# Two-layer attention, FFN and recurrence program on one core: one block of instructions for neighbouring stages, and activations turned into tiles during the last column chunk

## The chip, the cores and the metric

The program runs on one core of a Trainium2 chip. The metric is the device time of one execution in microseconds. Before the change it is 3304.31 us, the median of three runs (3301.08 to 3310.72).

## What is computed

A residual stream of 256 tokens by 2048 columns passes through six sub-layers. Two are the mixers of the older half (several kinds of attention, each with a memory projection), then come a grouped attention, a gated FFN, a recurrent mixer and a second gated FFN. Nearly all of the arithmetic is dense products with weights that are read once:

```
for each sub-layer:
    h = rms_norm(x, gain) @ w_in          # 2048 x (6680, 6224, 3072, 2*5632, 4096)
    y = mixer(h)                          # attention, recurrence, or silu(gate) * up
    x = x + y @ w_out                     # 2048 (5632 for the FFN) x 2048
```

The products are wanted at nearly float32 accuracy. So each activation a and each weight w is split into a high part (rounded) and a low part (the rest), and three products are added: a_hi w_hi + a_hi w_lo + a_lo w_hi.

## The kernel before

**Tiling.** `T` = 256 tokens are `MT` = 2 row blocks of 128. The 2048 inner columns are `KT` = 16 tiles of 128. A weight matrix is worked in column chunks of 512 (`CHUNK`). A granule is 1 MB of weights: four inner tiles by 512 columns (in the down projection one inner tile by 2048 columns). Four granules make a chunk. SyncE loads granules into four buffers (`load`, L333), ScalarE writes the high half (`split_hi`, L373) and VectorE the low half (`split_lo`, L385), each in two halves of 128x1024, into four slots (`HL` = 4). So the two engines are at most four halves ahead of TensorE. TensorE takes 24 matmuls of 512 columns a granule (L568 in `gemm`, L1689 in `ffn_up`, L1774 in `ffn_down`).

**Stages.** `build` (L148) runs one stage after another, each in an `nc.Block()` of its own, that is, with a wait of all engines for each other at its end: a key/value projection for the memory, then `gemm` with `evac="proj"` (in), a mixer, `gemm` with `evac="resid"` (out) three times; then `ffn_up` and `ffn_down`; then `gemm` with `evac="xy"`, `rnn_mixer`, `gemm` with `evac="resid"`; then `ffn_up`, `ffn_down` and `store_x`. At the end of each stage SyncE already loads the first four granules of the next (`prefetch`, L348).

**The head of a stage.** A stage that begins with a norm has `prep=Norm(...)` (L745, a `Turn`, L680). `Turn.tensor` (L693) runs ahead of the first chunk: 32 transposes of 128x128 (L698) of the residual into all eight PSUM banks, two tiles a bank. In the first chunk ScalarE (L721) and VectorE (L735) write for each granule first the high and low halves of four activation tiles, and then the two halves of the weights. The squares for the norm (L768) follow in granules 2 and 3 of the first chunk, and the row scale is applied when the chunk is read out of PSUM.

**The end of a stage.** A chunk's sums are read out (`evacuate`, L460) two granules into the next chunk; for the last chunk of a stage, after the last matmul. In the output projections VectorE does it as an addition to the residual (L478).

**The FFN.** `ffn_up` has eleven rounds f of a gate part (PSUM banks 0, 1) and an up part (banks 2, 3). ScalarE applies Silu, VectorE multiplies (`product`, L1621), TensorE turns the product with eight transposes (`turn`, L1657, L1664, banks 4, 5) after the third granule of the next round, and ScalarE copies them out (`copy_hidden`, L1589). The last round's product, transposes and copy stand at the end of the stage. `ffn_down` has eleven rounds j of four granules; it keeps all eight banks as sums of both row blocks by 2048 columns, splits the hidden tiles into high and low parts (L1743, L1752), and adds all 2048 columns of both row blocks to the residual at the very end (L1758). `store_x` (L669) then writes 2 MB with one DMA (L674).

Of the kernel before, what the change touches and what calls it, by code (L numbers as in the profile page):

```python
# [128 lines left out]


# [17 lines left out]
def build(nc, i, out, upto=99):  # L148
    ctx = ExitStack()
    with ctx:  # L150
# [121 lines left out]
        e.gran = 0  # L272
        e.queue = plan(e)
# [3 lines left out]
        gemm(e, evac="kv", prep=Norm(e, e.PR[:, :, 0:D], GC_MEM, loaded=e.s_mem))  # L277

        gemm(e, evac="proj", prep=Norm(e, e.X[:], GC_NORM, loaded=e.s_x), post=even_heads(e))
        gemm(e, evac="resid", prep=even_mixer(e))  # L280
        if upto > 1:
            gemm(e, evac="proj", prep=Norm(e, e.X[:], GC_NORM + KT), post=odd_heads(e))
            gemm(e, evac="resid", prep=odd_mixer(e))

        if upto > 2:
            gemm(e, evac="proj", prep=Norm(e, e.X[:], GC_MIX), post=gqa_heads(e))
            gemm(e, evac="resid", prep=gqa_mixer(e))
        if upto > 3:
            ffn_up(e, Norm(e, e.X[:], GC_FFN))
            ffn_down(e)  # L290
        if upto > 4:
            gemm(e, evac="xy", prep=Norm(e, e.X[:], GC_MIX + KT))
            rnn_mixer(e)
            gemm(e, evac="resid")
        if upto > 5:
            ffn_up(e, Norm(e, e.X[:], GC_FFN + KT))
            ffn_down(e)
        store_x(e)


# [47 lines left out]
def prefetch(e, sp):  # L348
# [4 lines left out]
    for q in range(4):  # L353
        if "down" in gm:
            load(e, sp, g0 + q, e.RAW[q][:], gm["down"][:, q, :], q)
        elif "rnn" in gm:
# [4 lines left out]
        else:  # L361
            one = gm.get("gate", gm)
            w = min(CHUNK, one["cols"])
            src = one["view"](0, q, w)
# [6 lines left out]


def split_hi(e, act, g, slot, rounds, n=GRAN):  # L373


    arrived(e, act, slot, rounds)
    for b in range(2):
        free = e.s_used.at(g * 2 + b - HL + 1)
        if not isinstance(g, int) or free > 0:
            act.wait_ge(e.s_used.sem, free)  # L380
        e.nc.scalar.activation(e.WH[(2 * slot + b) % HL][:, 0:n // 2], e.RAW[slot][:, b * n // 2:(b + 1) * n // 2],  # L381
                               ACT.Copy).then_inc(e.s_hi.sem, 1)


def split_lo(e, dve, g, slot, n=GRAN):  # L385

    for b in range(2):
        s = (2 * slot + b) % HL
        dve.wait_ge(e.s_hi.sem, e.s_hi.at(g * 2 + b + 1))
        e.nc.vector.tensor_tensor(e.WL[s][:, 0:n // 2], e.RAW[slot][:, b * n // 2:(b + 1) * n // 2],  # L390
                                  e.WH[s][:, 0:n // 2].bitcast(F32), ALU.subtract).then_inc(e.s_lo.sem, 1)
# [15 lines left out]
def chunk_loop(eng, n, body):  # L407


    for c in range(min(2, n)):  # L410
        body(c, c)
    pairs = (n - 2) // 2
    if pairs > 0:
        with eng.Fori(1, pairs + 1) as j:
            for h in range(2):
                body(j * 2 + h, h)
    if n > 2 and n % 2:
        body(n - 1, (n - 1) % 2)


def gemm(e, evac, prep=None, post=None):


    nc = e.nc
    gm = e.queue.pop(0)
    full, tail = gm["cols"] // CHUNK, gm["cols"] % CHUNK
    chunks = full + (1 if tail else 0)

    loop = post is None and evac != "kv"
    g0 = e.gran  # L430
    ktiles = 4

    with nc.Block() as block:
        @block.sync
        def _(sp):
            def body(c, par, w=CHUNK):
# [3 lines left out]
            if full:  # L440

                if full > 1:
                    body(1, 1)
                pairs = (full - 2) // 2
                if evac == "kv":
                    for c in range(2, full):
                        body(c, c % 2)
# [1572 lines left out]
```

## Time and profile before

| | |
|---|---|
| median of three runs | 3304.31 us |
| span of the profiled execution | 3299.8 us |
| TensorE busy | 3103.4 us, 94% |
| VectorE busy | 1727.6 us, 52% |
| ScalarE busy | 1519.2 us, 46% |
| DMA engines, share of their time in the main queue | 50.7% |
| granted TensorE clock, mean | 0.970 |

The profile lists engines as PE (TensorE's matmuls), PEld (its weight loads), DVE (VectorE), ACT (ScalarE), POOL (GpSimd) and SP (SyncE); a q behind the name is the engine's sequencer. L568 is line 568 of the kernel. Matmuls are pipelined, so a matmul's shown duration overlaps with the next one's: what one costs is the distance between two starts. A transpose is also a matmul for TensorE.

### The profile page before, as it was taken

The numbers are of one execution on the slowest core, as the hardware profiler recorded it, in microseconds if no ns is written. First come the engines' busy times: TensorE is split into PE (matmuls) and PEld (weight loads), VectorE is DVE, ScalarE is ACT, GpSimd is POOL, SyncE is SP. The second block draws the span as 40 slices with busy tenths as digits, with TensorE's granted clock in tenths as the row PEclk, the third lists the DMA queues.
The fourth block names the chain that finished last, engine by engine and source line by source line (L and its number), as shares of the span: only waits on it lengthen the run. The fifth ranks groups of instructions, "written<-read, shape, count | busy, mean of one in ns | idle before, by whom it ended". The sixth has DMA issues, their size and how long they took to land. (4 is left out here: it accounts for less than half of the span.)

```text
span 3299.8 us, 39116 instructions
## 1 busy us (share of the span) xinstructions
PE 3103.4 (94%) x14382; PEld 2574.4 (78%) x14382; DVE 1727.6 (52%) x2313; ACT 1519.2 (46%) x2117; POOL 273.1 (8%) x330
## 2 busy tenths in 40 slices
PE   6999988999979998999999999999739999999998
PEld 5888866888878887888888788788538888887887
DVE  4565537465456566544444455544585544444554
ACT  4545435354444545444444344443654444444443
POOL 0042200036000080000000000000110000000000
PEclk9999988999979999999999999999869999999999
DMA  7555431565514552555555555565225655565553
GB/s 254 179 191 191 153 131 39 167 203 192 170 54 141 179 191 66 178 191 190 191 190 179 178 191 192 168 198 181 77 71 172 197 187 187 187 197 166 192 195 134
DMA packets 253943, 551.62 MB, mean 167 GB/s; under 512 B 13232, under 2 KB 30480, under 8 KB 241808
## 3 DMA queue, kind: packets, MB, share of 16 engines
q1 hardware_dynamic: 252592, 548.84, 50.7%
q0 software_dynamic: 384, 1.05, 0.2%
q8 instruction: 61, 1.00, 0.1%
q10 hardware_dynamic: 864, 0.39, 0.0%
q14 instruction: 42, 0.34, 0.0%
HBM read 548.14 MB, written 2.10 MB: 167 GB/s over the span
## 5 line engine op out<-in xcount | busy, mean ns | idle before, releaser
L390 DVE TENSOR_TENSOR weights_lo<-weights,weights_hi 128x1024 fp32r<-128x1024 f32 (+1 forms) x1016 | 1232.8, 1222 | 1116.7 <-ACT weights_hi L381 1115.6
L381 ACT ACTIVATE weights_hi<-weights 128x1024 fp32r<-128x1024 f32 (+1 forms) x1016 | 1055.1, 1049 | 1246.1 <-PE psum L568 617.9
L568 PE MATMUL psum<-weights_hi,act_hi 128*128 128x512 f32 (+2 forms) x1952 | 757.3, 388 | 52.7 <-DVE weights_lo L390 52.7
L568 PE MATMUL psum<-weights_hi,act_lo 128*128 128x512 f32 (+2 forms) x1952 | 756.5, 388 | 0.0
L568 PE MATMUL psum<-weights_lo,act_hi 128*128 128x512 f32 (+2 forms) x1952 | 756.5, 388 | 0.0
L1689 PE MATMUL psum<-weights_hi,act_hi 128*128 128x512 f32 x1408 | 550.0, 391 | 1.8 <-DVE weights_lo L390 1.8
L1689 PE MATMUL psum<-weights_hi,act_lo 128*128 128x512 f32 x1408 | 548.3, 389 | 0.0
L1689 PE MATMUL psum<-weights_lo,act_hi 128*128 128x512 f32 x1408 | 547.7, 389 | 0.0
L568 PEld LDWEIGHTS psum<-weights_hi,act_hi 128*128 128x128 f32 x1952 | 371.9, 191 | 127.7 <-DVE weights_lo L390 49.9
L568 PEld LDWEIGHTS psum<-weights_lo,act_hi 128*128 128x128 f32 x1952 | 372.0, 191 | 73.4
L568 PEld LDWEIGHTS psum<-weights_hi,act_lo 128*128 128x128 f32 x1952 | 372.0, 191 | 73.4
L1689 PEld LDWEIGHTS psum<-weights_hi,act_hi 128*128 128x128 f32 x1408 | 264.3, 188 | 56.4 <-issue 2.2
L1689 PEld LDWEIGHTS psum<-weights_hi,act_lo 128*128 128x128 f32 x1408 | 264.3, 188 | 55.2
L1689 PEld LDWEIGHTS psum<-weights_lo,act_hi 128*128 128x128 f32 x1408 | 264.4, 188 | 54.3
L1774 PE MATMUL psum<-weights_hi,ffn_hidden_hi 128*128 128x512 f32 x704 | 275.8, 392 | 8.7 <-DVE weights_lo L390 8.7
L1774 PE MATMUL psum<-weights_lo,ffn_hidden_hi 128*128 128x512 f32 x704 | 275.2, 391 | 0.0
L1774 PE MATMUL psum<-weights_hi,ffn_hidden_lo 128*128 128x512 f32 x704 | 275.1, 391 | 0.0
L1774 PEld LDWEIGHTS psum<-weights_hi,ffn_hidden_hi 128*128 128x128 f32 x704 | 133.0, 189 | 36.9 <-DVE weights_lo L390 9.2
L1774 PEld LDWEIGHTS psum<-weights_hi,ffn_hidden_lo 128*128 128x128 f32 x704 | 133.0, 189 | 27.8
L1774 PEld LDWEIGHTS psum<-weights_lo,ffn_hidden_hi 128*128 128x128 f32 x704 | 133.1, 189 | 27.6
L927 POOL TENSOR_TENSOR rotation_temps<-proj,shape_consts 128x128 f32<-128x128 f32 (+3 forms) x100 | 80.2, 822 | 632.9 <-DVE proj L909 598.9
L1909 POOL TENSOR_TENSOR rnn_input<-rnn_input,rnn_conv 128x512 f32<-128x512 f32 x16 | 22.9, 1441 | 1148.0 <-ACT rnn_input L1878 1148.0
(222 smaller groups left out, 1965.1 us busy)
## 6 DMA issues: line engine op xcount, KB each, us to landing
weights<-in_ffn_w_gate SPq DMA_DIRECT2D x88, 1024.0 KB, 5.2
weights<-in_ffn_w_up SPq DMA_DIRECT2D x88, 1024.0 KB, 5.1
weights<-in_ffn_w_down SPq DMA_DIRECT2D x88, 1024.0 KB, 4.8
weights<-in_even_w_in SPq DMA_DIRECT2D x52, 1024.0 KB, 5.0
weights<-in_odd_w_in SPq DMA_DIRECT2D x48, 1024.0 KB, 5.1
weights<-in_w_out SPq DMA_DIRECT2D x32, 1024.0 KB, 5.1
weights<-in_rnn_w_in SPq DMA_DIRECT2D x32, 1024.0 KB, 5.3
weights<-in_attn_w_qkv SPq DMA_DIRECT2D x24, 1024.0 KB, 5.2
```

The source lines that it names most:

```text
L381: e.nc.scalar.activation(e.WH[(2 * slot + b) % HL][:, 0:n // 2], e.RAW[slot][:, b * n // 2:(b + 1) * n // 2], ACT.Copy).then_inc(e.s_hi.se ...
L390: e.nc.vector.tensor_tensor(e.WL[s][:, 0:n // 2], e.RAW[slot][:, b * n // 2:(b + 1) * n // 2], e.WH[s][:, 0:n // 2].bitcast(F32), ALU.subt ...
L568: last = nc.tensor.matmul(e.PS[:, 2 * par + m, 0:w], a, x, start=(kk == 0 and n == 0), stop=(kk == 4 * ktiles - 1 and n == 2))
L927: mult = lambda out, a, b: e.nc.gpsimd.tensor_tensor(out, a, b, ALU.mult)
L1689: last = nc.tensor.matmul(e.PS[:, 2 * part + m, :], a, x, start=(kk == 0 and j == 0), stop=(kk == KT - 1 and j == 2))
L1774: last = nc.tensor.matmul(e.PS[:, 4 * m + 2 * h + b, :], a, x, start=(first and k == 0), stop=(final and k == 2))
L1909: nc.gpsimd.tensor_tensor(mine(e.RIX, g), mine(e.RIX, g), of(e.XC, n), ALU.mult).then_inc(e.s_input.sem, 1)
```

## The change

What is done at the joints between stages is rearranged; the products are the same.

- Stages that have no mixer between them share one `nc.Block()` (class `Flow`): kv and even in; even out and odd in; odd out and qkv; attention out, FFN up, FFN down and recurrent in; recurrent out, FFN up, FFN down and the store. Signals are read through marks (`Mark`) taken when a stage is made, so that a stage's waits stay valid while the next one is being written.
- `gemm` becomes the class `Gemm`. Its chunk loops are written out. The last chunk's read-out moves to the next stage, after its second granule (`carry_scalar`, `carry_vector`).
- The 32 transposes of the next norm go in four portions of eight (`CHUNK_LEAD`): after granules 0, 1 and 2 of the last chunk of the stage before, and after granule 1 of the new stage's first chunk. They use banks 4 to 7 twice. The high and low halves of the activations follow on ScalarE and VectorE: two groups in the last chunk, two in the new stage's first. Each portion waits for the addition of its residual columns, and for its bank's former contents to be split.
- The last round's product, transposes and copy of the FFN's up stage move into the down stage's first granule (`carry_tensor` and the others), which uses other PSUM banks first.
- The down stage's last two granules are loaded as two inner tiles by 1024 columns each. So the left 1024 columns are finished 24 matmuls before the end, and are added then (`add(dve, 0)`); the right ones are added in the next stage (`add(dve, 1)`). The next norm's transposes go in four portions: after the first and the second half of the right columns' matmuls, and after granules 0 and 1 of the next stage (`HALF_LEAD`).
- The store is four DMAs of 512 columns, each after the addition of its columns.

The core of the diff:

```diff
+        flow = Flow(e)
+        flow.add(Gemm, evac="resid", prep=turned)
+        flow.add(FfnUp, prep=Norm(e, e.X[:], GC_FFN, lead=CHUNK_LEAD))
+        flow.add(FfnDown)
+        flow.add(Gemm, evac="xy", prep=Norm(e, e.X[:], GC_MIX + KT, lead=HALF_LEAD))
+        flow.emit()
+        rnn_mixer(e)
...
+    def vector(self, dve):
+        mine = self.kind == "resid"
+        prep, post = self.prep, self.post
+        for c, w in enumerate(self.widths):
+            for q in range(4):
+                if c == 0 and prep is not None:
+                    prep.before_lo(dve, q)
+                self.split_lo(dve, c * 4 + q, q, 4 * w)
+                if q == 1 and c > 0 and mine:
+                    self.evacuate(dve, c - 1)
+                if q == 1 and c == 0 and self.prev is not None:
+                    self.prev.carry_vector(dve)
+                if c == 0 and prep is not None:
+                    prep.after_lo(dve, q)
+                if post is not None:
+                    post.vector(dve, c - 1, q)
+                if c == self.last and self.next is not None:
+                    self.next.prep.early_lo(dve, q)
...
+CHUNK_LEAD = Lead((4, 5, 6, 7, 4, 5, 6, 7), {0: 0, 1: 1, 2: 2}, {2: 0, 3: 1}, {1: 3}, {0: 2, 3: 3})
+HALF_LEAD = Lead((6, 7, 6, 7, 4, 5, 6, 7), {}, {}, {0: 2, 1: 3}, {0: 0, 1: 1, 2: 2, 3: 3})
...
+    def turn(self, pe, q):
+
+        e = self.e
+        for k in range(4 * q, 4 * q + 4):
             self.ready(pe, k)
+            b = k // 2
+            before = [x for x in range(b) if self.banks[x] == self.banks[b]]
+            if k % 2 == 0 and before:
+                pe.wait_ge(self.alo.sem, self.alo.at(before[-1] + 1))
...
     def ready(self, pe, k):
...
+        if k % 4 == 0:
+            pe.wait_ge(*self.final[k // 4])
...
+    BANK = ((0, 2), (6, 4))
...
+                    for m in range(MT):
+                        if first and h == 0 and m == 0:
+                            pe.wait_ge(up.gate.sem, up.gate.at(up.n))
+                        if first and h == 1 and m == 0:
+                            up.carry_tensor(pe)
+                        if first and h == 1 and m == 1:
+                            pe.wait_ge(up.hcopied.sem, up.hcopied.at(up.n))
+                        last = self.products(None, h, m, hh, hl, q, (2 * q + h) % HL, 0, first)
...
+        for h in range(2):
+            for k in range(2):
+                pe.wait_ge(self.lo.sem, self.lo.at(final * 8 + (2 + h) * 2 + k + 1))
                 for m in range(MT):
...
+                    last = self.products(None, h, m, hh, hl, 2 + k, (2 * (2 + h) + k) % HL, 0, final=(k == 1))
+                last.then_inc(self.used.sem, 1)
+                if h == 1 and self.next.prep is not None:
+                    self.next.prep.turn(pe, k)
...
+        for q in range(4):
+            cols = slice(q * CHUNK, (q + 1) * CHUNK)
+            sp.wait_ge(*self.final[q])
+            sp.dma_start(dst[:, :, cols], e.X[:, :, cols]).then_inc(self.out.sem, 16)
+        sp.wait_ge(self.out.sem, self.out.at(4))
```

The four dictionaries of a `Lead` are: granule of the old stage's last chunk to portion transposed, the same for the activation halves, and both for the new stage's first chunk.

## Rows read from the trace of the kernel before

**Rows 1.** Page, busy us of each engine, share of the span, instructions.
```profile
PE 3103.4 (94%) x14382; PEld 2574.4 (78%) x14382; DVE 1727.6 (52%) x2313; ACT 1519.2 (46%) x2117; POOL 273.1 (8%) x330
```

**Rows 2.** TensorE's waits: who for whom, us in total, times, longest us.
```profile
PE psum L568 <- DVE weights_lo L390: 52.7, 5, 49.5
PE psum L636 <- DMA cmp_w<-in_nsa_cmp_w: 22.0, 1, 22.0
...
PE psum L1774 <- DVE weights_lo L390: 8.7, 2, 4.4
...
PE psum L698 <- PEq L433: 7.9, 5, 1.6
...
PE psum L698 <- PEq L1723: 4.8, 1, 4.8
...
PE psum L1664 <- DVE ffn_hidden L1629: 3.0, 2, 1.5
```

**Rows 3.** Timeline, TensorE at the joint before the second FFN: start, duration, instruction, [idle].
```profile
2544.45 0.39 PE L568 MATMUL psum<-weights_hi,act_lo 128*128 128x512 f32 x1
2544.67 0.39 PE L568 MATMUL psum<-weights_hi,act_hi 128*128 128x512 f32 x1
...
2545.13 0.39 PE L568 MATMUL psum<-weights_hi,act_lo 128*128 128x512 f32 x1
2547.09 3.69 PE L698 MATMUL psum<-shape_consts,resid 128*128 128x128 f32 x32 [1.58 <-PEq L433]
2551.68 0.47 PE L1689 MATMUL psum<-weights_hi,act_hi 128*128 128x512 f32 x1 [0.90 <-DVE weights_lo L390]
```

**Rows 4.** Timeline, VectorE and ScalarE at the same joint.
```profile
2545.55 1.22 DVE L478 TENSOR_TENSOR resid<-resid,psum 128x1024 f32<-128x1024 f32 x1 [8.56 <-PE psum L568]
2548.64 1.66 DVE L735 SCALAR_TENSOR_TENSOR act_lo<-psum,gain_cols,act_hi 128x256 fp32r<-128x256 f32 x4 [1.87 <-ACT act_hi L721]
2550.31 2.36 DVE L390 TENSOR_TENSOR weights_lo<-weights,weights_hi 128x1024 fp32r<-128x1024 f32 x2
...
2547.77 1.57 ACT L721 ACTIVATE act_hi<-psum,gain_cols 128x256 fp32r<-128x256 f32 x4 [12.04 <-PE psum L698]
2549.21 2.02 ACT L381 ACTIVATE weights_hi<-weights 128x1024 fp32r<-128x1024 f32 x2
...
2558.41 1.89 ACT L768 ACTIVATE squares<-resid 128x2048 bf16<-128x2048 f32 x1
2560.22 0.18 ACT L768 ACTIVATION_READ_ACCUMULATOR squares<-resid 128x1 f32 x1
```

**Rows 5.** Timeline, TensorE where the FFN's loop turns a hidden chunk.
```profile
1446.91 1.04 PE L1664 MATMUL psum<-shape_consts,ffn_hidden 128*128 128x128 f32 x8
1447.71 0.47 PE L1689 MATMUL psum<-weights_hi,act_hi 128*128 128x512 f32 x1
1448.02 0.39 PE L1689 MATMUL psum<-weights_lo,act_hi 128*128 128x512 f32 x1
```

**Rows 6.** Timeline, TensorE from the first FFN's up to its down stage.
```profile
1874.83 0.39 PE L1689 MATMUL psum<-weights_hi,act_lo 128*128 128x512 f32 x1
1876.72 1.09 PE L1664 MATMUL psum<-shape_consts,ffn_hidden 128*128 128x128 f32 x8 [1.50 <-DVE ffn_hidden L1629]
1882.17 0.80 PE L1774 MATMUL psum<-weights_hi,ffn_hidden_hi 128*128 128x512 f32 x1 [4.36 <-DVE weights_lo L390]
...
1886.54 0.40 PE L1774 MATMUL psum<-weights_lo,ffn_hidden_hi 128*128 128x512 f32 x1
```

**Rows 7.** The same in the second FFN.
```profile
3046.91 0.80 PE L1774 MATMUL psum<-weights_hi,ffn_hidden_hi 128*128 128x512 f32 x1 [4.36 <-DVE weights_lo L390]
...
3050.46 0.40 PE L1774 MATMUL psum<-weights_hi,ffn_hidden_lo 128*128 128x512 f32 x1
```

**Rows 8.** Busy time by stretch, with the granted clock: up to down, and inside recurrent in.
```profile
core 0: us, PE busy (x) PEld busy (x) DVE busy (x) ACT busy (x) POOL busy (x), PEclk, DMA share, GB/s
1875.00:1889.00 14.00, 8.14 (x30) 6.36 (x30) 7.35 (x10) 6.90 (x9) 0.00 (x0) 0.76 0.33 116
...
2133.00:2160.00 27.00, 27.00 (x126) 22.49 (x125) 18.84 (x27) 22.15 (x32) 0.00 (x0) 1.00 0.64 199
```

**Rows 9.** Timeline, VectorE and ScalarE from up to down.
```profile
1875.25 1.41 DVE L1629 SCALAR_TENSOR_TENSOR ffn_hidden<-psum,rstd,ffn_gate 128x512 f32<-128x512 f32 x2 [8.56 <-PE psum L1689]
...
1877.85 1.02 ACT L1592 ACTIVATE ffn_hidden_t<-psum 128x1024 f32<-128x1024 f32 x1 [12.41 <-PE psum L1664]
```

**Rows 10.** Timeline, TensorE from the first down stage to recurrent in.
```profile
2123.45 0.39 PE L1774 MATMUL psum<-weights_hi,ffn_hidden_lo 128*128 128x512 f32 x1
2128.67 5.35 PE L698 MATMUL psum<-shape_consts,resid 128*128 128x128 f32 x32 [4.82 <-PEq L1723]
2133.77 0.48 PE L568 MATMUL psum<-weights_hi,act_hi 128*128 128x512 f32 x1
```

**Rows 11.** Timeline, VectorE at the same joint.
```profile
2123.88 4.48 DVE L1758 TENSOR_TENSOR resid<-resid,psum 128x2048 f32<-128x2048 f32 x2 [8.56 <-PE psum L1774]
```

**Rows 12.** Timeline of the end, all engines.
```profile
3287.78 0.39 PE L1774 MATMUL psum<-weights_hi,ffn_hidden_lo 128*128 128x512 f32 x1
3288.21 4.48 DVE L1758 TENSOR_TENSOR resid<-resid,psum 128x2048 f32<-128x2048 f32 x2 [8.56 <-PE psum L1774]
3292.94 0.40 SPq L674 DMA_DIRECT2D out_resid<-resid  x1
```

**Rows 13.** DMAs from 3292 to 3300 us: 40 slices of 0.2 us; issues with us to landing.
```profile
DMA  0000000009699499496895993994995968000000
...
out_resid<-resid SPq DMA_DIRECT2D x1, 2048.0 KB, 6.4
```

More of the change, by code:

```diff
@@ L145, with build @@
     pass
-def build(nc, i, out, upto=99):
+def build(nc, i, out):
     ctx = ExitStack()
@@ new lines, with __init__, add, emit @@
+class Flow:
+    def __init__(self, e):
+        self.e, self.stages = e, []
+    def add(self, kind, **args):
+        prev = self.stages[-1] if self.stages else None
+        stage = kind(self.e, prev, **args)
+        if prev is not None:
+            prev.next = stage
+        self.stages.append(stage)
+    def emit(self):
+        e = self.e
+        with e.nc.Block() as block:
+            @block.sync
+            def _(sp):
+                for stage in self.stages:
+                    stage.sync(sp)
+                prefetch(e, sp)
+            @block.scalar
+            def _(act):
+                for stage in self.stages:
+                    stage.scalar(act)
+            @block.vector
+            def _(dve):
+                for stage in self.stages:
+                    stage.vector(dve)
+            @block.gpsimd
+            def _(pool):
+                for stage in self.stages:
+                    stage.pool(pool)
+            @block.tensor
+            def _(pe):
+                for stage in self.stages:
+                    stage.tensor(pe)
@@ L837, in __init__ @@
         self.e, self.funcs = e, funcs
+        self.evac, self.square, self.hsquare, self.hmean, self.hroot, self.hnorm = (
+            s.mark() for s in (e.s_evac, e.s_square, e.s_hsquare, e.s_hmean, e.s_hroot, e.s_hnorm))
         n = (cols + CHUNK - 1) // CHUNK
@@ new lines, in product, with carry_vector @@
+    def product(self, dve, f):
+        e = self.e
+        dve.wait_ge(self.used.sem, self.used.at(f * 16 + 16))
+        dve.wait_ge(self.gate.sem, self.gate.at(f + 1))
+        if not isinstance(f, int) or f > 0:
+            dve.wait_ge(self.hturned.sem, self.hturned.at(f))
+        for m in range(MT):
+            ins = e.nc.vector.scalar_tensor_tensor(e.HID[:, m, :], e.PS[:, 2 + m, :], e.RS[:, m:m + 1], e.GATE[:, m, :], ALU.mult, ALU.mult)
+        ins.then_inc(self.hid.sem, 1)
+    def carry_vector(self, dve):
+        self.product(dve, self.n - 1)
@@ new lines, in vector, with body @@
+    def vector(self, dve):
+        for q in range(4):
+            self.split_lo(dve, q, q)
+            if q == 1:
+                self.prev.carry_vector(dve)
+            self.prep.after_lo(dve, q)
+        for q in range(4):
+            self.split_lo(dve, 4 + q, q)
+        def body(f):
+            for q in range(4):
+                self.split_lo(dve, f * 8 + q, q)
+                if q == 1:
+                    self.product(dve, f - 1)
+            for q in range(4):
+                self.split_lo(dve, f * 8 + 4 + q, q)
+        body(1)
+        with dve.Fori(2, self.n) as f:
+            body(f)
@@ new lines, in turn @@
+    def turn(self, pe, f, first):
+        e = self.e
+        pe.wait_ge(self.hid.sem, self.hid.at(f + 1))
+        if not first:
+            pe.wait_ge(self.hcopied.sem, self.hcopied.at(f))
+        for k in range(4):
+            for m in range(MT):
+                last = e.nc.tensor.transpose(e.PS[:, 4 + k // 2, (k % 2) * T + m * P:(k % 2) * T + (m + 1) * P],
+                                             e.HID[:, m, k * P:(k + 1) * P], e.CT[:, 0:P])
+        last.then_inc(self.hturned.sem, 1)
```

905 lines of the change are left out of this document (473 added, 432 removed).

## The prediction

> **What bounds the kernel now.** I read the page first: TensorE is busy for 3103.4 of 3299.8 us, VectorE for 52% and ScalarE for 46% [rows 1]. So only time in which TensorE stands still, runs at a low clock or does extra work can be won. The second view is the list of TensorE's waits [rows 2]. Most of the idle time belongs to places that the change leaves alone: 49.5 us ahead of the output projection of the recurrent mixer, 22.0 us for the constants at the start, the gated products, the mixers' own waits. What belongs to joints without a mixer is small: 7.9 us in five waits for the end of a block, 4.8 us in one, 8.7 us in two waits for the first weights of a down projection, 3.0 us in two for the last hidden chunk, and some waits of 0.9 us for weights.
>
> The third view is the timeline at each kind of joint, and it gives the sum. A steady matmul costs 0.23 us from start to start (2544.45 to 2544.67 [rows 3]); the overlapping durations of 0.39 us are not the cost. The nine joints are: key/value projection to even projection, even output to odd projection, odd output to qkv projection, attention output to first FFN, recurrent output to second FFN (five alike, "kind A"); up to down projection (two, "kind B"); first down projection to recurrent input projection (one, "kind C"); second down projection to the store (one, "kind D").
>
> **Kind A, five joints.** The last matmul of the old stage starts at 2545.13 and the first of the new one at 2551.68 [rows 3]: 6.55 us, less the 0.23 of the matmul itself, 6.32. In it lie 1.58 us of waiting for the block's end, 3.69 us of 32 transposes, and 0.90 us for the first weights, because ScalarE and VectorE must serve the new activations before the new weights [rows 4]. The change doesn't remove the transposes: they are TensorE's own work, now in four portions of eight between granules. What a portion costs in that position is shown inside the FFN: eight transposes from 1446.91 to 1447.71, and then one pitch of 0.31 in place of 0.23 [rows 5], 0.88 us in all. Four cost 3.52. Gain: 6.32 - 3.52 = 2.80 a joint, 14.0 us for five. That the five are alike I take from the 7.9 us in 5 waits [rows 2].
>
> What must cover it: in the old stage's last chunk VectorE has per granule (5.4 us of TensorE, 24 matmuls) two weight halves of 1.2 us and, where it turns activations, 1.65 us more; at the second granule it has an addition of 1.22 us instead [rows 4]. That is at most 4.1 of 5.4 us. ScalarE has two halves of 1.0 and 1.6 us of activation halves, or a square of 1.89 + 0.18 us; both together come only in the last granule of the new stage's first chunk, 5.7 us, and it gets its weights ahead by a granule. The new wait that matters is TensorE's wait for the addition of the old stage's last chunk, ahead of the fourth portion. It stands two granules (10.9 us) after the last matmul of the old stage; VectorE needs one weight half after ScalarE's (1.0 + 1.2) and the addition (1.2), 3.5 us, and is free of the joint by then. Behind that wait on TensorE stands every later matmul, so cover lost here would cost one for one.
>
> **Kind B, two joints.** From 1874.83 to 1882.17 [rows 6], 7.34 - 0.23 = 7.11 us. The eight hidden transposes stay (0.88), so 6.23 a joint, 12.5 for two. Then the clock: in both joints TensorE stood still for 1.50 and 4.36 us, and the next matmuls start every 0.43 us: ten intervals from 1882.17 to 1886.54 take 4.37 instead of 2.27 us [rows 6], and eight from 3046.91 to 3050.46 take 3.55 instead of 1.82 [rows 7]. That is 2.1 + 1.7 = 3.8 us lost at the lower level, 1.2 of 2.4 GHz (mean granted clock 0.76 over the stretch [rows 8]). With no such idle time I count it as won. Does a new stall come? The new order starts the first six-by-two matmuls (2.7 us) in banks that the gate's Silu has freed, then turns the hidden chunk, then needs its copy only for the last six. VectorE's product takes 1.41 us from 0.4 us after the last matmul's start, so it is done a microsecond before the transposes want it. The copy takes 1.02 us [rows 9] beside six matmuls of 1.36 us: with semaphore delays a stall of 0 to 0.3 us. I take 0. Kind B: 16.3 us.
>
> **Kind C, one joint.** From 2123.45 to 2133.77 [rows 10], 10.32 - 0.23 = 10.09 us, of which four portions stay: 10.09 - 3.52 = 6.57. The new order finishes the left 1024 columns of both row blocks first, 24 matmuls (5.4 us) before the end; VectorE adds them while 12 matmuls (2.7 us) run, and then the first transposes read them. Two additions of 1024 columns take half of 4.48 us, from about 0.43 us after the last left matmul's start [rows 10, 11], so about 0.2 us after its slot ends: 0.2 + 2.24 = 2.5 of 2.7 us. This cover is thin, and so is the next: from the end of the left columns VectorE has 2.5 (addition) + 2.4 (first weights) + 1.7 (first activations) = 6.6 us, while TensorE comes to the new stage after 5.4 + 2 x 0.88 = 7.2. If ScalarE's part is in the way instead, 0 to 3 us are lost. I take 0 because both sums come out under their cover.
>
> **Kind D, the end.** From the last matmul's start (3287.78) to the end of the span are 12.0 us: 0.43 to the additions, 4.48 for them, 0.25 to the store's issue, 0.86 to its first bytes, 5.0 for 2.1 MB, 0.5 to 1.0 for the rest [rows 12, 13]. Afterwards only the right half is left behind the last matmul: 0.43 + 2.24 + 0.25 + 0.86 + 2.5 + 1.0 = 7.3 us, 7.4 with some of the second issue. Gain 4.6. Bounds: if a half moves no quicker than the whole did, 2.2; if the left half's store were no burden and 0.4 of the issue were hidden, 5.1. The Trainium skill (DMA: Bandwidth & Descriptors, the section with the two cost components of a DMA) gives each DMA some 2.0 us fixed and the rest by bytes at 436 GB/s. By that the two stores of 0.52 MB behind the end would take 2.0 + 2.4 = 4.4 us from issue to landing where mine says 3.9, and the sum would be 0.5 us smaller; no row of before has so small a store.
>
> **The rest.** The projections that were loops (recurrent input, the output projections) are written out. Their cost in the loop is nil: in 2133 to 2160 us, inside the new stage, TensorE is busy for all 27.0 us at clock 1.00 [rows 8]. The Trainium skill (Runtime: NRT & Kernel Launch, Instruction fetch mechanics) says that a taken branch can force a fetch, so that writing loops out should pay; the rows show no idle time there and I count zero. The loads' order is the same; the down projection's last two granules come in half as wide pieces, which matters only if a load is late, and none is waited for at a joint [rows 2]. On SP's queue, the next stage's loads no longer stand behind a block's end, with nothing waiting for them.
>
> **Sum.** 14.0 + 16.3 + 6.6 + 4.6 = 41.5 us. The profiled execution spans 3299.8 us and the median of the runs shown is 3304.3, 4.5 more; I subtract from the median: 3304.3 - 41.5 = 3262.8 us (a span of 3258.3).
>
> **The rivals.** *First: the portions cost more between matmuls than in the FFN's loop.* 24 portions are new in their places. If each waits some 0.6 us for a semaphore or a bank, 14 us come back and the time is 3277. For it: a portion after idle time took 1.09 us [rows 6], and the kind C covers are thin. Against it: the loop's portion also waits for two engines and shows no idle time [rows 5]. *Second, the one that ends slower: TensorE's queue is in order.* A portion that waits for VectorE's addition or for a bank holds back all matmuls, and these free the weight buffers that VectorE and ScalarE need, so the wait could feed itself: VectorE does its weight halves ahead of the addition in its own order. It decides from 1.8 us a portion (24 x 1.8 = 43), and at 2.7 us, the time of half a granule, it would give 3304 - 41 + 65 = 3328. Against it: VectorE and ScalarE are busy half of the time and have a granule of lead. The Trainium skill (TensorE: Matmul & The Clock Gate, Step-by-step) says that matmuls stay in program order and only weight loads are pulled ahead; that is this mechanism, and no row of before shows a portion late. *Third: it doesn't do what it says*, because the joints only move the idle time to the second granule (VectorE's backlog of new weights, additions and activations, 3 to 5 us at each of eight joints): only the store, the clock and about 3 us a kind B joint are won, 15 us, 3289. Against it: the rows behind today's joints show no idle time on TensorE even though all the 16 tiles' halves fall there (27.0 busy of 27.0 us [rows 8]).
>
> **How the numbers follow.** The forecast has 0.75, the first rival 0.15, the third 0.06, the second 0.04. 0.3% is 10 us, about what a measurement of this kernel can tell from no change. The range reaches from 3254 (half a portion's cost hidden, 10 us less by 24 x 0.4) to 3276 (the first rival almost whole, with 2.4 us lost in the store and 3 in kind C on the way). Faster by over 0.3%: the forecast, the first and nearly all of the third, 0.94. Same: 0.03. Slower: 0.03.
>
> **What would show each step.** Right: at the five kind A joints no wait of TensorE over 0.15 us and portions of eight transposes of 0.8 to 0.9 us; at the two kind B joints no clock under 1.00 and eight transposes after twelve matmuls of the down projection; at kind C no wait ahead of the first portion; after the last matmul about 7.4 us. Wrong: waits of TensorE at the transposes' line for the addition or for the activations' low halves, or waits of the first matmuls of new stages for weights that VectorE has behind other work. What would break the forecast most is a self-feeding wait at the portions, or mixers that start later than now.

## The result, and the profile after

The changed kernel takes 3263.13 us (median of four runs, 3260.72 to 3266.48), beside 3307.51 us for the kernel before in the same comparison: ratio 0.9871, 95% interval 0.9857 to 0.9884. A second comparison gave 3266.32 and 0.9867 (0.9850 to 0.9883). The forecast was 3262.8. The profiled execution spans 3263.1 us, 36.7 less than that of before; the forecast for it was 3258.3. So the median agreed to 0.4 us and the span missed by 4.8 us; both need an explanation.

The list of TensorE's waits, first lines and all that concern activations or weights (who for whom, us in total, times, longest):

```profile
PE psum L627 <- DVE weights_lo L477: 50.3, 2, 49.8
PE psum L688 <- DMA cmp_w<-in_nsa_cmp_w: 21.8, 1, 21.8
PE psum L792 <- DVE proj L940: 15.0, 2, 10.9
...
PE psum L792 <- PEq L644: 3.0, 1, 3.0
...
PE psum L792 <- PEq L1217: 0.7, 1, 0.7
```

L627 are the matmuls of the projections, L1832 and L1960 those of the FFN's up and down stages, L792 the transposes of the activations and L1801 those of the hidden chunks. L469 and L477 write the high and the low half of the weights, L1947 is the down stage's addition. Of [rows 2] the lines of the joints are gone: five waits of 7.9 us, one of 4.8, two of 8.7, two of 3.0. What is left of the first line is the wait behind the recurrent mixer (49.8, before 49.5) and one of 0.5 us at the head of another output projection.

The timeline of TensorE at the joint before the second FFN (start, duration, instruction), which answers to [rows 3]: the third portion, the joint itself, the fourth portion.

```profile
2520.80 1.03 PE L792 MATMUL psum<-shape_consts,resid 128*128 128x128 f32 x8
2521.59 0.48 PE L627 MATMUL psum<-weights_hi,act_hi 128*128 128x512 f32 x1
2521.91 0.40 PE L627 MATMUL psum<-weights_lo,act_hi 128*128 128x512 f32 x1
...
2526.90 0.39 PE L627 MATMUL psum<-weights_hi,act_lo 128*128 128x512 f32 x1
2527.13 0.39 PE L1832 MATMUL psum<-weights_hi,act_hi 128*128 128x512 f32 x1
...
2538.01 1.03 PE L792 MATMUL psum<-shape_consts,resid 128*128 128x128 f32 x8
2538.80 0.48 PE L1832 MATMUL psum<-weights_hi,act_hi 128*128 128x512 f32 x1
```

At 2527.13 the stage changes, and the distance is the 0.23 of any two matmuls. A portion costs 0.79 us and one pitch (distance of two starts) of 0.32 in place of 0.23, as in [rows 5]. Measured in the same way, all 24 portions of the trace cost 0.88 or 0.89 us.

The same for the joints of kind B (first FFN, up to down, [rows 6]) and C (down to recurrent in, [rows 10]); the ACT row is ScalarE's copy of the hidden chunk, the DVE row VectorE's addition of the left half:

```profile
1867.90 0.39 PE L1832 MATMUL psum<-weights_hi,act_lo 128*128 128x512 f32 x1
1868.13 0.39 PE L1960 MATMUL psum<-weights_hi,act_hi 128*128 128x512 f32 x1
...
1870.86 1.03 PE L1801 MATMUL psum<-shape_consts,ffn_hidden 128*128 128x128 f32 x8
1871.65 0.48 PE L1960 MATMUL psum<-weights_hi,act_hi 128*128 128x512 f32 x1
...
1871.93 1.03 ACT L1723 ACTIVATE ffn_hidden_t<-psum 128x1024 f32<-128x1024 f32 x1 [2.54 <-PE psum L1801]
...
2103.17 2.35 DVE L1947 TENSOR_TENSOR resid<-resid,psum 128x1024 f32<-128x1024 f32 x2 [3.12 <-PE psum L1960]
...
2105.70 1.04 PE L792 MATMUL psum<-shape_consts,resid 128*128 128x128 f32 x8
2106.49 0.48 PE L1960 MATMUL psum<-weights_hi,act_hi 128*128 128x512 f32 x1
...
2109.32 1.03 PE L792 MATMUL psum<-shape_consts,resid 128*128 128x128 f32 x8
2110.11 0.48 PE L627 MATMUL psum<-weights_hi,act_hi 128*128 128x512 f32 x1
```

At kind B come twelve matmuls, eight transposes and more matmuls, with no idle time and no pitch of 0.43 us, the one of the lower clock in [rows 6]. The copy is done at 1872.96 and the matmuls that wait for it start at 1873.11. At kind C the addition ends at 2105.52 and the transposes that read it start at 2105.70. That was the thin cover of the forecast (2.5 of 2.7 us), and it held by 0.2 us.

The end (SPq: SyncE issues a DMA), which answers to [rows 12]:

```profile
3255.74 0.39 PE L1960 MATMUL psum<-weights_hi,act_lo 128*128 128x512 f32 x1
...
3256.17 2.35 DVE L1947 TENSOR_TENSOR resid<-resid,psum 128x1024 f32<-128x1024 f32 x2 [3.09 <-PE psum L1960]
3258.55 0.89 SPq L735 DMA_DIRECT2D out_resid<-resid  x2
```

From the last matmul's start to the end of the span it is 7.36 us (forecast 7.4, before 11.98).

**Where the time went, by stretch.** Distances between the first matmuls of the stages, in us:

| stretch | before | after | difference | forecast |
|---|---|---|---|---|
| start to first projection | 31.09 | 31.55 | +0.46 | 0 |
| kv and even in | 393.91 | 390.90 | -3.01 | -2.8 |
| even mixer | 138.70 | 141.78 | +3.08 | 0 |
| even out and odd in | 371.89 | 369.02 | -2.87 | -2.8 |
| odd mixer | 78.25 | 78.27 | +0.02 | 0 |
| odd out and qkv | 231.43 | 228.63 | -2.80 | -2.8 |
| grouped attention | 48.21 | 49.61 | +1.40 | 0 |
| out, FFN, recurrent in (A, B, C) | 1016.24 | 998.09 | -18.15 | -17.7 |
| recurrent mixer | 146.98 | 146.59 | -0.39 | 0 |
| out, FFN (A, B) | 831.08 | 821.30 | -9.78 | -10.8 |
| end | 11.98 | 7.36 | -4.62 | -4.6 |

The stretches that the change touches gained 41.2 us, where 41.5 were forecast. Of the 4.8 us that the span lacks, the other 4.6 lie in the start and the mixers, whose work is the same.

### The profile page after: what moved, and what is told of

It reads as the page before. It is cut to its first block and busy times, and to the rows that moved or that the text cites. A ratio compares the mean times of both kernels' runs of the same rounds, so it can differ in the third digit from the quotient of the medians.

```text
span 3263.1 us, 38217 instructions
## 1 busy us (share of the span) xinstructions
PE 3100.6 (95%) x14382; PEld 2575.2 (79%) x14382; DVE 1730.2 (53%) x2317; ACT 1521.7 (47%) x2117; POOL 273.7 (8%) x330
## 5 line engine op out<-in xcount | busy, mean ns | idle before, releaser
L477 DVE TENSOR_TENSOR weights_lo<-weights,weights_hi 128x1024 fp32r<-128x1024 f32 (+1 forms) x1016 | 1234.6, 1222 | 1166.2 <-ACT weights_hi L469 1164.8
L469 ACT ACTIVATE weights_hi<-weights 128x1024 fp32r<-128x1024 f32 (+1 forms) x1016 | 1055.6, 1048 | 1302.1 <-PE psum L627 658.6
L627 PE MATMUL psum<-weights_hi,act_hi 128*128 128x512 f32 (+2 forms) x1952 | 759.1, 389 | 50.3 <-DVE weights_lo L477 50.3
L627 PE MATMUL psum<-weights_lo,act_hi 128*128 128x512 f32 (+2 forms) x1952 | 757.2, 388 | 0.0
L627 PE MATMUL psum<-weights_hi,act_lo 128*128 128x512 f32 (+2 forms) x1952 | 757.1, 388 | 0.0
L1832 PE MATMUL psum<-weights_hi,act_hi 128*128 128x512 f32 x1408 | 549.6, 390 | 0.0
L1832 PE MATMUL psum<-weights_hi,act_lo 128*128 128x512 f32 x1408 | 547.9, 389 | 0.0
L1832 PE MATMUL psum<-weights_lo,act_hi 128*128 128x512 f32 x1408 | 547.8, 389 | 0.0
L627 PEld LDWEIGHTS psum<-weights_hi,act_hi 128*128 128x128 f32 x1952 | 372.1, 191 | 123.4 <-DVE weights_lo L477 50.2
L627 PEld LDWEIGHTS psum<-weights_hi,act_lo 128*128 128x128 f32 x1952 | 372.3, 191 | 74.2
L627 PEld LDWEIGHTS psum<-weights_lo,act_hi 128*128 128x128 f32 x1952 | 372.3, 191 | 73.2
L1832 PEld LDWEIGHTS psum<-weights_hi,act_lo 128*128 128x128 f32 x1408 | 264.4, 188 | 54.8
L1832 PEld LDWEIGHTS psum<-weights_hi,act_hi 128*128 128x128 f32 x1408 | 264.4, 188 | 54.1
L1832 PEld LDWEIGHTS psum<-weights_lo,act_hi 128*128 128x128 f32 x1408 | 264.4, 188 | 54.0
L1960 PE MATMUL psum<-weights_hi,act_hi 128*128 128x512 f32 x704 | 274.2, 389 | 0.0
L1960 PE MATMUL psum<-weights_hi,act_lo 128*128 128x512 f32 x704 | 273.9, 389 | 0.0
L1960 PE MATMUL psum<-weights_lo,act_hi 128*128 128x512 f32 x704 | 273.9, 389 | 0.0
L1960 PEld LDWEIGHTS psum<-weights_hi,act_hi 128*128 128x128 f32 x704 | 132.2, 188 | 27.5 <-ACT ffn_hidden_t L1723 0.3
L1960 PEld LDWEIGHTS psum<-weights_lo,act_hi 128*128 128x128 f32 x704 | 132.2, 188 | 27.5
L1960 PEld LDWEIGHTS psum<-weights_hi,act_lo 128*128 128x128 f32 x704 | 132.2, 188 | 27.3
```

The lines of the kernel that those rows point to most:

```text
L627: last = e.nc.tensor.matmul(e.PS[:, banks.start + m, 0:w], a, x, start=(kk == 0 and n == 0), stop=(kk == KT - 1 and n == 2))
L1832: last = e.nc.tensor.matmul(e.PS[:, 2 * part + m, :], a, x, start=(kk == 0 and j == 0), stop=(kk == KT - 1 and j == 2))
L1960: last = e.nc.tensor.matmul(e.PS[:, self.BANK[m][h] + b, :], a, x, start=(first and k == 0), stop=(final and k == 2))
```

## The experiments

All are variants of the changed kernel, unless it is said otherwise. The comparisons by stretch use the table above.

**A block for each stage again.** Left out is only the sharing of a block; down and recurrent in stay together. `head` issues the next stage's first four loads.

```diff
-        with e.nc.Block() as block:
...
+            if groups and isinstance(groups[-1][-1], FfnDown) and isinstance(stage, Gemm):
+                groups[-1].append(stage)
+            else:
+                groups.append([stage])
+        for n, group in enumerate(groups):
+            group[0].headed = True
+            with e.nc.Block() as block:
...
+                    if n + 1 < len(groups):
+                        groups[n + 1][0].head(sp)
```

> The changed kernel with a block of its own for every stage again, at seven of the eight joints inside the flows and ahead of the store; only down to recurrent in stays in one block. The first four granules are loaded in the block before, all early portions of transposes stay. Theory (what is won is the preparing of the new stage's first weights while TensorE still works on the old one): at each of the five joints of kind A TensorE waits 1.6 us for the block's end, then 1.06 for the high and 1.2 us for the low half of the first weights, about 4.0 us; at the two of kind B the hidden tile's halves of 0.4 us each come on top, 4.7 us, and the clock may fall as it did before, 2 us each; the end is 1.6 us longer. Together +31 us without a fall of the clock, up to +40 with it at several joints: 3294 to 3303 us. Rival (the block's end costs only the wait that the profile of before gives it, 1.6 us): 8 times 1.6, +13 us, 3276 us.

Measured: 3292.27 us, 0.9951 of before (0.9935 to 0.9967); span 3290.6, 27.5 more than the changed kernel and less than the 31 to 40 expected; 26.7 of it lie in the stretches with joints and in the end. Waits of TensorE, and the joint before the second FFN:

```profile
PE psum L646 <- DVE weights_lo L491: 58.5, 5, 49.6
...
PE psum L1990 <- DVE weights_lo L491: 6.6, 2, 3.3
PE psum L1858 <- DVE weights_lo L491: 5.6, 2, 2.8
```

```profile
2542.90 0.39 PE L646 MATMUL psum<-weights_hi,act_lo 128*128 128x512 f32 x1
2543.64 2.00 ACT L483 ACTIVATE weights_hi<-weights 128x1024 fp32r<-128x1024 f32 x2 [10.46 <-PEq L425]
2544.73 2.36 DVE L491 TENSOR_TENSOR weights_lo<-weights,weights_hi 128x1024 fp32r<-128x1024 f32 x2 [10.18 <-ACT weights_hi L483]
...
2546.10 0.47 PE L1858 MATMUL psum<-weights_hi,act_hi 128*128 128x512 f32 x1 [2.82 <-DVE weights_lo L491]
```

The mechanism is the theory's: ScalarE starts at the block's end, VectorE behind its first half, TensorE behind VectorE's first. The size was too high: 2546.10 - 2542.90 - 0.23 = 2.97 us a joint of kind A, not 4.0, because the block's end costs 0.74 - 0.23 = 0.5 us here (2542.90 to 2543.64, less the matmul's own pitch) and not 1.6. The 1.58 us of [rows 3] contained the last addition, 1.22 us [rows 4], which now is done elsewhere. The waits for weights are 58.5 - 49.6 = 8.9 us in four (one of them, of 0.5 us, the changed kernel has too), 5.6 in two and 6.6 in two. After them the clock stood at its lower level in three places (2547 to 2550 us among them). Joints and clock together made the two FFN stretches 8.4 and 9.4 us longer. The rival's 13 us are excluded: the blocks cost twice that, though their own waiting (eight times about 0.5) is a seventh of it.

**All portions of kind A behind the last matmul or later.**

```diff
-CHUNK_LEAD = Lead(..., {0: 0, 1: 1, 2: 2}, {2: 0, 3: 1}, {1: 3}, {0: 2, 3: 3})
+CHUNK_LEAD = Lead(..., {3: 0}, {}, {0: 2, 1: 3}, {0: 0, 1: 1, 2: 2, 3: 3})
...
                     self.next.prep.early_tensor(pe, q)
+                    if q == 3:
+                        self.next.prep.turn(pe, 1)
```

> One block, but at the five joints of kind A no portion of transposes before the last matmul of the old stage: portions 0 and 1 stand right behind it, 2 and 3 behind granules 0 and 1 of the new stage. Theory (the early portions only have to be early enough for ScalarE and VectorE to write the first activation halves): TensorE waits after its 1.6 us of transposes for two high halves and two low halves behind them, about 3.1 us after the last matmul, so 1.4 us of idle time a joint, +7 us, a wait for act_lo. Rival (the placing of the portions is what won the time at kind A, 2.8 us each): +14 us. Second rival (the block's end alone): 0.

Span 3274.6, +11.5. At the joint before the second FFN:

```profile
2533.91 1.91 PE L794 MATMUL psum<-shape_consts,resid 128*128 128x128 f32 x16
2537.13 0.50 PE L1834 MATMUL psum<-weights_hi,act_hi 128*128 128x512 f32 x1 [1.31 <-DVE act_lo L864]
```

and in the list of waits:

```profile
PE psum L627 <- DVE act_lo L864: 3.9, 3, 1.3
...
PE psum L1834 <- DVE act_lo L864: 2.6, 2, 1.3
```

Five waits of 1.3 us, 6.5 in all, with the releaser that the theory named (it said 7). The other 5 us aren't at the joints: 1.3 us each lie in the narrow last chunk of the even and the odd projection (the even one's last 96 matmuls took 17.4 us here and 16.1 in the changed kernel), 1.0 in the start, most of the rest in the mixers. They needn't be the edit's: in the second profile of the unaltered changed kernel the same 96 matmuls took 17.5 us. So at kind A the early portions are worth 1.3 of the 2.8 us. That the other 1.5 come from weights prepared early and from the addition moved away is argued: no run moves the addition alone, and the separate blocks cost 2.97 us a joint with the early portions kept, so the parts overlap and can't be added up.

**Every portion twice.**

```diff
+                for again in range(1 if self.lead is None else 2):
+                    last = e.nc.tensor.transpose(e.PS[:, self.banks[b], (k % 2) * T + m * P:(k % 2) * T + (m + 1) * P],
+                                                 self.tile(k, m), e.CT[:, 0:P])
```

> Every one of the 24 interleaved portions is transposed twice, the same result into the same place. Theory (a portion costs TensorE its own time in full and nothing else): eight more transposes of 0.10 us, 0.80 us a portion, +19 us, with no waits at the joints. Rival (portions lie in time that TensorE has spare, as the words of the change may suggest): under +5 us. Rival (the covers are thin, so that later portions make ScalarE, VectorE and with them TensorE late): more than +25 us and waits of TensorE for weights or activations near the joints.

Span 3281.1, +18.0, and no wait at a joint:

```profile
2536.63 1.91 PE L793 MATMUL psum<-shape_consts,resid 128*128 128x128 f32 x16
2538.30 0.47 PE L627 MATMUL psum<-weights_hi,act_hi 128*128 128x512 f32 x1
```

Sixteen transposes take 1.67 us where eight took 0.79, so 0.88 us a portion. The stretches that hold portions grew by 22.6 us (24 x 0.88 = 21.1, most of the rest in the narrow last chunks), and the even mixer was 3.8 us shorter this time. A portion is TensorE's own time in full, and both rivals are excluded. How thin the covers are this doesn't test: a doubled portion gives its results 0.9 us later, and TensorE comes to need them 0.9 us later too.

**The hidden tail at the end of up again.**

```diff
-    def carry_scalar(self, act):
-        self.copy_hidden(act, self.n - 1)
...
+        self.copy_hidden(act, self.n - 1)
...
-    def carry_vector(self, dve):
-        self.product(dve, self.n - 1)
...
+        self.product(dve, self.n - 1)
...
     def carry_tensor(self, pe):
-        self.turn(pe, self.n - 1, False)
+        pass
...
+        self.turn(pe, self.n - 1, False)
```

> One block, but the last round's product, transposes and copy of the FFN's up stage stand at that stage's end again, on all three engines, and not in the down stage's first granule. Theory (what kept TensorE waiting at kind B was ScalarE's queue order: copy, then hidden tile, then weights): TensorE waits 1.5 us for the product and, after 0.9 us of transposes, some 4.1 us for weights, because ScalarE holds the first weights back behind the copy: +5.6 us a joint, plus up to 2 us for the clock, +11 to +16 us. Rival (it was the block's end): only the 1.5 us ahead of the transposes come back, +3 us for the two.

The three added calls stand at the end of `FfnUp.scalar`, `vector` and `tensor`. Span 3280.0, +16.9, a little above the range expected; the two FFN stretches grew by 8.7 and 7.9 us. TensorE and then ScalarE from up to down:

```profile
1869.40 0.39 PE L1830 MATMUL psum<-weights_hi,act_lo 128*128 128x512 f32 x1
...
1871.29 1.09 PE L1799 MATMUL psum<-shape_consts,ffn_hidden 128*128 128x128 f32 x8 [1.50 <-DVE ffn_hidden L1766]
1876.34 0.80 PE L1959 MATMUL psum<-weights_hi,act_hi 128*128 128x512 f32 x1 [3.96 <-DVE weights_lo L477]
...
1872.42 1.02 ACT L1723 ACTIVATE ffn_hidden_t<-psum 128x1024 f32<-128x1024 f32 x1 [12.41 <-PE psum L1799]
1873.34 0.41 ACT L1896 ACTIVATE act_hi<-ffn_hidden_t 128x256 fp32r<-128x256 f32 x1
1873.65 1.99 ACT L469 ACTIVATE weights_hi<-weights 128x1024 fp32r<-128x1024 f32 x2
```

6.94 - 0.23 - 0.88 = 5.83 us (said: 5.6), with no block's end in it. ScalarE stood idle for 12.41 us, because the copy is ahead of the down stage's weights in its program. In the changed kernel it writes the first of these weights at 1860.23 us, 7.9 us before the down stage's first matmul. The kernel before lost 6.23 us a joint, so its block's end added 0.4 us on top of what the order of the work costs. The two prices don't add up: with the tail moved away, the separate blocks cost 3.5 us here. The clock fell again in both FFNs (1875 to 1882 us in the first), which is the rest, 2.9 and 2.0 us.

**One store.**

```diff
-        for q in range(4):
...
-            sp.dma_start(dst[:, :, cols], e.X[:, :, cols]).then_inc(self.out.sem, 16)
...
+        sp.wait_ge(*self.final[3])
+        sp.dma_start(dst, e.X[:]).then_inc(self.out.sem, 16)
...
```

> The store is one DMA of 2 MB again, behind the addition of the right half. Theory (the left half's bytes move under the last matmuls): after the last matmul's start 0.43 + 2.35 + 0.25 us to the issue and 6.4 + 0.46 to the end as in the kernel before, 9.9 us where the changed kernel has 7.35, +2.5 us. Rival (the gain at the end came from the shorter additions alone): 0.

```profile
3257.77 0.39 PE L1958 MATMUL psum<-weights_hi,act_lo 128*128 128x512 f32 x1
3258.19 2.35 DVE L1945 TENSOR_TENSOR resid<-resid,psum 128x1024 f32<-128x1024 f32 x2 [3.09 <-PE psum L1958]
3260.57 0.39 SPq L733 DMA_DIRECT2D out_resid<-resid  x1
```

The span is 3267.4, so from the last matmul's start to the end it is 9.61 us, +2.25. The addition lasts 2.35 us, as in the changed kernel, where the kernel before needed 4.48. So of the 4.6 us at the end, half are bytes moved early and half the additions of half the width. The rival's 0 is excluded.

**The left half added at the end.**

```diff
-        dve.wait_ge(self.used.sem, self.used.at(2 * FT - 2 + 2 * h))
+        dve.wait_ge(self.used.sem, self.used.at(2 * FT))
...
-                if h == 1 and self.next.prep is not None:
-                    self.next.prep.turn(pe, k)
+        if self.next.prep is not None:
+            self.next.prep.turn(pe, 0)
+            self.next.prep.turn(pe, 1)
```

So the portions 0 and 1 stand behind the last matmul.

> In both down stages the left half is added only when all matmuls are done, and the first two portions of transposes of the recurrent input stand behind that. Theory (the split of the last granules is what pays at kind C): the addition takes 0.43 + 2.35 us from the last matmul's start, then come transposes, ScalarE's and VectorE's first activation halves behind the first weights: TensorE idles some 2.5 us before the transposes and 2.5 us behind them, +5 us, and the end is 2.6 us longer because the stores of the left half begin later: +7.6 us. Rival (the block's end was the price at kind C): 0 there, and only the 2.6 us at the end.

```profile
2111.96 1.09 PE L792 MATMUL psum<-shape_consts,resid 128*128 128x128 f32 x8 [2.45 <-DVE resid L1947]
2115.11 1.94 PE L792 MATMUL psum<-shape_consts,resid 128*128 128x128 f32 x8 [2.05 <-DVE act_lo L862]
2116.70 0.78 PE L627 MATMUL psum<-weights_hi,act_hi 128*128 128x512 f32 x1
2117.27 0.63 PE L627 MATMUL psum<-weights_lo,act_hi 128*128 128x512 f32 x1
```

The stretch of the first FFN grew by 7.5 us (5 expected) and the end by 2.8 (to 10.15), the span by 11.3. The idle times are 2.45 and 2.05 us; the second is a wait of portion 1, which shares its banks with portion 0, and not of the first matmuls as I had said. Most of the rest is the clock: the matmuls from 2117.27 start 0.43 us apart. The rival (nothing at kind C) is excluded.

**The right half added in two steps ahead of the store.** This is the version that the end pointed to.

```diff
...
+        for n in range(2):
+            for m in range(MT):
+                x = e.X[:, m, (2 + n) * CHUNK:(3 + n) * CHUNK]
+                ins = e.nc.vector.tensor_tensor(x, x, e.PS[:, self.prev.BANK[m][1] + n, :], ALU.add)
+            ins.then_inc(self.quarter.sem, 1)
```

> The right half is added in two steps of 512 columns ahead of the store, so that the third of the four stores starts after the first. Theory (at the end the additions and the bytes stand in a row, and can overlap): third store issued 1.1 us earlier, the last one 0.2 later, its bytes done some 0.8 us earlier: the time from the last matmul's start to the end is 6.5 in place of 7.35 us. Rival (the last DMA's own latency sets the end): 7.5 us, no gain. No difference is expected that the median can tell; the trace tells it.

```profile
3255.58 0.39 PE L1969 MATMUL psum<-weights_hi,act_lo 128*128 128x512 f32 x1
3256.01 2.48 DVE L750 TENSOR_TENSOR resid<-resid,psum 128x512 f32<-128x512 f32 x4 [3.09 <-PE psum L1969]
3257.32 1.57 SPq L738 DMA_DIRECT2D out_resid<-resid  x2
```

The third store is issued 1.74 us after the last matmul's start, where the changed kernel needs 2.81. The end is 6.27 us (the span is 3261.9), 1.09 less than in the changed kernel, a little more gain than said. The median is 3263.59 (3259.44 to 3264.0), 0.9860 of before (0.9843 to 0.9876), beside 0.9867 (0.9850 to 0.9883) of the unaltered changed kernel in the same comparison. It has the shortest span of all profiled executions, and by the medians it can't be told from the changed kernel.

**The changed kernel again, and the kernel before twice.** No edit.

> The changed kernel once more. Theory (the 5 us by which the profiled span missed the forecast lie in the mixers, by the clock, and not in the joints): the nine joints last what they did to 0.2 us, and the stretch from the compression's first matmul to the even output projection lasts either 136 us, with about 24 us at half clock at its end, or 140 us, with about 30, the same two values as in the other kernels. Rival (written-out loops or the earlier end of the stage make the mixers slower): always 140 us.

> The kernel before, unchanged, profiled again. The changed kernel and seven of its eight variants took 49.6 us or a little less in the grouped attention and about 142 us in the stretch from the compression to the even output projection, where the profiled execution of before took 48.2 and 138.7. Theory (which of the two values comes is a matter of where the clock's fall meets the stretch, in any kernel): the kernel before shows the longer values too in some executions, and its span is then 4 us or more above 3299.8. Rival (written-out loops or the joined stages make the mixers slower): it shows 138.7 and 48.2 again, within 0.5 us.

> The kernel before, unchanged, a further execution, for the same question: theory, at least one of these two shows an even mixer stretch of about 142 us with some 30 us at half clock at its end; rival, both show 138.7 us with 24.

The changed kernel's joints came out the same to 0.2 us, but for the first stretch, 392.28 instead of 390.90, which is the narrow chunk. The gains of four rows of the table repeat likewise: odd out and qkv took 231.43 to 231.45 us in the three profiles of before and 228.63 in both of the changed kernel, the first FFN's stretch 1016.1 to 1017.3 and 998.1, the second's 831.1 and 821.3, the end 11.98 and 7.36. Its even mixer took 142.06 (the expectation's 136 and 140 count from the compression's first matmul, some 2 us later than the table). The kernel before took 142.04 and 143.22 us there and 48.4 and 49.7 in the grouped attention, with spans of 3303.1 and 3308.1. Busy times by stretch for the even mixer (us; busy of PE, PEld, DVE, ACT, POOL; granted clock, DMA share, GB/s): the profile of before, the kernel before again, the changed kernel, and the kernel with every portion twice:

```profile
425.02:563.71 138.69, 116.04 (x734) 87.27 (x734) 78.42 (x328) 59.54 (x198) 2.34 (x1) 0.88 0.19 62
...
424.53:567.75 143.22, 120.56 (x734) 91.07 (x734) 79.49 (x329) 60.59 (x199) 2.34 (x1) 0.84 0.18 60
...
422.46:564.24 141.78, 119.13 (x734) 90.22 (x734) 79.04 (x328) 60.12 (x199) 2.34 (x1) 0.85 0.18 60
...
427.11:565.13 138.02, 115.36 (x733) 86.88 (x734) 78.34 (x328) 59.43 (x198) 2.34 (x1) 0.88 0.19 62
```

The work is the same 734 matmuls (one record is missing in the last row). In all four TensorE is idle for the same 22.65 us, to 0.01; only its busy time moves, and with it the granted clock. The rival, that the longer values are the change's doing, falls with the two further profiles of before. Over all kernels here the stretch lasted 138.0 and 138.7 us in the two profiles where its last fall of the clock lasted 24 us, and 141.8 to 143.3 in the others, where it lasted 31. In the grouped attention the granted clock is 0.97 at 48.2 and 48.4 us and 0.94 at 49.6 and 49.7. What decides between the values in an execution stays open, and so does whether the change makes one of them likelier: the changed kernel and its four variants with the same joints up to there all took 49.6 to 49.7 us in the grouped attention.

## Why the prediction was right, and where it was off

**The sum.** Joints and end: 41.5 us said, 41.2 found. By kind: A, three stretches, 8.4 said, 8.7 found; A, B and C together 17.7 and 18.2; the end 4.6 and 4.62. Of the three of kind A only the last, 2.80 us, is clean. The other two hold the narrow last chunks, and they lasted 392.8 to 393.9 and 371.3 to 374.1 us in the profiles of before, 390.9 to 392.3 and 368.9 to 369.0 in those of the changed kernel. The second FFN's stretch gave 9.8 for 10.8; its first 312 matmuls lost 3.0 us to the low clock behind the recurrent mixer, while the whole output stage of before lost 1.6, so 1.4 us are the clock's and the joints gave 11.1. That the loops written out cost and win nothing was right as well: the 768 matmuls of recurrent in took 173.96 us before and 175.74 after, with two portions of 0.88 among them. The upper bound of the range, 3276, doesn't follow from its parts: 14 + 2.4 + 3 us on top of 3262.8 are 3282.

**The step on the median.** I subtracted the sum from the median, and this is why 3262.8 came out. For the 4.5 us between median and span I gave no reason and carried them over, and that was wrong: a run's time is its span plus 1.8 us in all that list both, so the other 2.7 us were the difference between executions. The profiled execution of before (3299.8) had the shorter mixers, where the two further ones span 3303.1 and 3308.1, and that of the changed kernel (3263.1) had the longer ones, as its second had (3264.5). So the median gained 43 to 44 us and the two profiled spans 36.7, for the same 41 us of change. The runs of either kernel scatter over 6 to 10 us, and with the clock: of eight runs of before, the shortest span, 3300.0, has a mean granted clock of 0.971 and the longest, 3309.2, has 0.966. The hit to 0.4 us is in part luck. I started from a median of 3304.31, which one more run of before made 3307.51; from that the same sum would have given 3266.0.

**The terms that were mis-sized in their parts.** In kind A the 1.58 us were called a wait for the block's end; the separate blocks show the end alone at 0.5 us, and the rest of it was the last addition, which ran until 2546.77 [rows 4]. The term was right only because I took the whole distance between the matmuls and not the labels in it. In kind B the same holds: the label "first weights" hid ScalarE's queue order, which the hidden tail's return showed at 5.83 us without any block. The covers held: 0.2 us left at the first portion of kind C, and 0.15 us behind the hidden copy at kind B, where a stall of 0 to 0.3 us had been allowed.

**The rivals.** Portions dearer than in the loop: 0.88 us was said, and all 24 cost that. The self-feeding wait: none appeared, not even with the portions doubled. Idle time that moves to later granules: none; the stretches gained in full, each with the granules behind its joints.

**The end's DMA.** From the third store's issue to the landing of the fourth I had 3.9 us from the rows, and the trace shows 4.16 (3258.55 to 3262.71). From that issue to the end of the span I had 4.4 us, and it is 3263.1 - 3258.55 = 4.55, with an issue 0.2 us earlier after the addition than before. By the rule of the Trainium skill (DMA: Bandwidth & Descriptors, Anatomy of one DMA), 2.0 us fixed and the bytes at 436 GB/s, the landing is estimated at 4.4 us. The page gives that rule for DMAs that GpSimd issues, and here SyncE issues them; the measured 4.16 lies between it and my 3.9.

## What to carry to other kernels

At a stage boundary, count the whole distance between the last and the first matmul and compare it with the work that must stay; the profile's labels of the waits inside it name only the last releaser. A barrier's own cost was half a microsecond here, and 3.0 us a joint with what follows from it: the engines that prepare operands restart empty behind it. What paid was to let them prepare the new stage's first pieces before the old stage ends, and to put pieces that wait long, such as the hidden copy, behind these in the engine's program. Before reading a few microseconds of difference between two profiled spans, compare the stretches whose code is the same.

## What was not expected of the hardware

The even mixer's stretch, the same 734 matmuls, took 138.0 to 143.3 us over twelve profiles, with TensorE's idle time the same and its busy time longer where the granted clock was lower (0.84 to 0.88 over the stretch). With separate blocks, an idle time of about 3 us in front of new matmuls was followed by a fall of the clock at one joint of kind A (before the second FFN, 2547 to 2550 us) and by none at the four other joints of that kind. The narrow last chunk of the even projection (its last 96 matmuls) took 15.2 to 17.5 us over the twelve profiles. The granted clock falls to its lower level inside it in all of them, and its mean over the chunk was 0.64 where it took 16.1 us and 0.58 where it took 17.5. What makes the fall come sooner or later stays open.
